# Hybrid trunk step with PEER experts: six slots for expert rows, eleven weight chunk buffers in one pool, and four heads' queries of layer 1 made a pass later

## The chip, the cores and the metric

The kernel runs on one core of a Trainium2 chip, in fp32. The metric is device time in microseconds (us), the median of the runs.

## The reference

Two token groups go through two layers: 256 prompt tokens and 32 sample tokens (8 sequences of 4), width 1024. Layer 0 mixes with a gMLP, layer 1 with a short convolution; each is followed by a PEER feed-forward, which is where most of the data comes from.

```
# layer 0 mixer                           # layer 1 mixer
z = gelu(x @ w_in); u, v = split(z)        B, C, h = split(x @ w_in)
v = layer_norm(v)                          z = C * h
y = (u * (tril(w_s) @ v + b_s)) @ w_out    y = (B * conv3(z)) @ w_out

# PEER, each layer, per token
q = (x @ w_query).reshape(8 heads, 2, 128)
s = q . sub_keys                           # 2 x 128 scores a head
top 16 of each half -> 256 sums -> top 16 -> idx = i1 * 128 + i2;  g = softmax
a = gelu(expert_u[idx] . x)                # 16 rows of 1024 a head
y = sum(g * a * expert_v[idx])
```

Before each mixer and each feed-forward stands an RMS norm, with a residual sum behind; a last norm follows. The outputs are the 288 rows, layer 0's normalised v of the sample rows, and the convolution buffers.

## The kernel before, in words

**Tiles and items.** The tokens are three tiles: 128, 128 and 32 rows. For a token, a head and one of its 16 experts the kernel needs one row of u and one of v, which lie side by side in DRAM (2048 floats). An *item* is one such row for each of the 128 partitions: one indirect load of 1 MiB, issued by GpSimd (POOL), L717. A tile of 128 tokens has 8 x 16 = 128 items, the small tile, folded four times over the partitions, 32; two layers make 576 items. An item goes into slot n % RING of `uvring`. VectorE multiplies its first half with the normed token and sums (`dot`, L1485), ScalarE takes gelu, multiplies by the gate and scales a small diagonal matrix (`weigh`, L1090 to L1102, in one of DIAGS places), TensorE adds the second half, so weighted, into two PSUM banks (`weigh`, L764, 4 matmuls, which the trace records as 8; L756 for the small tile). POOL loads item n into its slot when item n - RING is through TensorE (`v_tensor`). At a tile's end the sums are added to x (L1501) before TensorE starts the next tile's first item.

**Chunks and passes.** The dense matrices are cut in chunks of 1024 x 256 floats, 1 MiB each, numbered in the order of use: pass 0 is layer 0 for tile 0 (chunks 0 to 31), pass 1 layer 0 for tiles 1 and 2 (32 to 63), pass 2 and pass 3 the same for layer 1 (64 to 87 and 88 to 111). In layer 0 a pass has eight chunks for v, eight for u, eight for the output projection and eight for the queries; in layer 1 twelve for B, C and h, four for the output and eight for the queries. SyncE (SP) issues the chunk loads in that order, one after the other, L661 in `load_chunk`, each when the last use of its place is over. `plan_homes` gives each chunk a place: during pass 0 slots of the row ring that no item needs yet, later a ring of two buffers, `wring`. Six chunks of each layer have a place in `kept`; they are loaded in the layer's first pass and used again in its second. TensorE waits in `chunk(n, c)` for the landing. `blocks` makes 128 columns of a result transposed (eight matmuls, 16 records of the trace; a chunk serves two blocks): u, L775 at 160 or 128 tokens, the convolution's three parts (`bch`) and the queries (`q`), which go to `qT` in `arena`. The scores of a group of four half heads (`s`, L952) are made of `qT` and the sub-keys; ScalarE copies them to `scores` when VectorE has scanned the scores of the tile before at that place (`scanned`).

**The order.** `mixer_steps` lists the dense steps of a pass with costs in us and with what each must follow. `plan_steps` deals them to *turns*: turn p is item p, and each engine has so much room in a turn for such steps (`ROOM`, by layer and tile of the item); routing steps (the top-16 search on VectorE, `route`) have due turns (`due`, which depends on RING). Each engine runs, turn by turn, its item's work and the steps dealt to the turn. What stands at turn -1 runs ahead of all items: pass 0 with the first scores. So the order on each engine is fixed before the run; only semaphores decide when.

## Time and profile before

| what | value |
|---|---|
| runs | 1755.15, 1756.94, 1757.65 us, median 1756.94 |
| span of the profiled execution | 1753.3 us (its own time is not given; the median stands 3.6 us above the span) |
| TensorE busy | 1323.9 us (76%) |
| VectorE busy | 1082.8 us (62%) |
| ScalarE busy | 659.9 us (38%) |
| GpSimd busy | 626.8 us (36%) |
| moved by DMA | 719.43 MB, mean 410 GB/s |
| mean granted TensorE clock | 0.811 |
| chain that ended last | DMA 52%, TensorE 28%, VectorE 6%, ScalarE 6% |

Busy shares are averages over stages with different limits: what a change is worth in a stage is read from the stretches of the trace. In the chain of work that ended last, each piece is either work or the flight of a DMA; a row load's piece reaches from its issue to its landing and holds the time it stands behind other loads. TensorE's instructions are pipelined, so a busy TensorE need not be one at its peak.

### The profile page before, as it was taken

Reading aid. Unit: us, or ns where it says so; the run is one execution under the profiler, and the core shown is the slowest. Engines: PE = TensorE matmul, PEld = TensorE weight load, DVE = VectorE, ACT = ScalarE, POOL = GpSimd, SP = SyncE. Lnnn points to the kernel's source line nnn. Section 1 sums busy time; section 2 is a strip of 40 time slices with the busy share of each in tenths; the row PEclk is TensorE's granted clock in tenths of the full one; section 3 lists DMA queues with packets and bytes.
Section 4 is the critical chain, followed back from the end, with each engine's and each line's share of the span. In section 5 each row is a group of like instructions: output and inputs, shape, how many; then the busy total and the mean of one; then the engine's idle time right before and its main releaser. Section 6 shows DMA issues by size and latency. Waiting matters only on the chain.

```text
span 1753.3 us, 23627 instructions
## 1 busy us (share of the span) xinstructions
PE 1323.9 (76%) x8378; PEld 638.9 (36%) x8378; DVE 1082.8 (62%) x2636; ACT 659.9 (38%) x2139; POOL 626.8 (36%) x580
## 2 busy tenths in 40 slices
PE   8999998998868777886654688687896666766634
PEld 6995554654535433441110255244441111111100
DVE  1358578555755566556677756677567766666454
ACT  2125444234434223343443533336343433433343
POOL 0014333333333223333343443343344444434442
PEclk9999998998989978987655699898886766666755
DMA  9979999999999999999999999999999999999997
GB/s 346 412 328 403 410 421 421 421 421 421 408 422 421 421 420 421 421 419 421 422 411 421 395 421 421 421 420 414 421 397 419 421 421 421 421 421 416 422 410 301
DMA packets 101478, 719.43 MB, mean 410 GB/s; under 512 B 12272, under 2 KB 13040, under 8 KB 14416
## 3 DMA queue, kind: packets, MB, share of 16 engines
q0 software_dynamic: 82944, 604.02, 83.3%
q1 hardware_dynamic: 17616, 113.17, 15.8%
q8 instruction: 66, 1.08, 0.2%
q10 hardware_dynamic: 800, 0.74, 0.1%
q14 instruction: 52, 0.43, 0.1%
HBM read 716.36 MB, written 1.52 MB: 409 GB/s over the span
## 4 chain that ended last, share of the span: by engine, by line
DMA 52%; PE 28%; DVE 6%; ACT 6%; issue 3%; SPq 2%; POOL 1%; DVEq 0%; ACTq 0%; POOLq 0%
DMA uvring<-expert_uv_dram,idx 51%; PE psum L764 11%; PE psum L775 8%; DVE uvring L1485 5%; PE psum L931 4%; ACT diag L1102 1%; PE psum L819 1%; ACT wgt L1098 1%; POOL uvring L717 1%; DMA wring<-w_chunks_dram 1%; SPq L674 1%; ACT a_gelu L1090 1%; ACT L1090 1%; PE psum L952 1%; PE psum L783 1%
## 5 line engine op out<-in xcount | busy, mean ns | idle before, releaser
L1485 DVE SCALAR_TENSOR_TENSOR uvring<-uvring,xn 128x1024 f32<-128x1024 f32 x576 | 705.1, 1225 | 547.0 <-DMA uvring<-expert_uv_dram,idx 534.4
L717 POOL DMA_INDIRECT uvring<-expert_uv_dram,idx x576 | 626.6, 1088 | 1105.1 <-PE psum L764 845.8
L764 PE MATMUL psum<-uvring,diag 64*64 64x512 f32 x4096 | 685.0, 762 | 305.6 <-ACT diag L1102 281.6
L1090 ACT ACTIVATE a_gelu<-a_raw 128x1 f32<-128x1 f32 x576 | 116.6, 202 | 880.0 <-DVE uvring L1485 861.9
L764 PEld LDWEIGHTS psum<-uvring,diag 64*64 64x64 f32 x4096 | 131.8, 155 | 733.5 <-ACT diag L1102 630.8
L775 PEld LDWEIGHTS psum<-xT,wring 128*128 128x128 f32 x1408 | 188.3, 195 | 66.4 <-issue 59.8
L775 PE MATMUL psum<-xT,wring 128*128 128x160 f32 (+1 forms) x1408 | 206.4, 301 | 3.1 <-DMA wring<-w_chunks_dram 3.1
L1102 ACT ACTIVATE diag<-twin,wgt 128x64 f32<-128x64 f32 x512 | 178.1, 348 | 48.9 <-PE psum L764 1.5
L1098 ACT ACTIVATE wgt<-a_gelu,gate 128x1 f32<-128x1 f32 x576 | 169.7, 295 | 20.9
L756 PE MATMUL psum<-uvring,diag 128*32 128x256 f32 x512 | 67.2, 630 | 95.3 <-ACT diag L1102 83.7
L775 PEld LDWEIGHTS psum<-xT,kept 128*128 128x128 f32 x576 | 75.6, 197 | 24.2 <-issue 24.2
L775 PE MATMUL psum<-xT,kept 128*128 128x128 f32 (+1 forms) x576 | 82.1, 299 | 0.0
L756 PEld LDWEIGHTS psum<-uvring,diag 128*32 128x32 f32 x512 | 13.3, 142 | 149.2 <-ACT diag L1102 134.9
L931 PE MATMUL psum<-wring,arena 128*128 128x256 f32 x272 | 64.5, 392 | 2.0 <-DMA wring<-w_chunks_dram 2.0
L981 ACT ACTIVATE arena<-psum 128x128 f32<-128x128 f32 (+2 forms) x152 | 42.9, 282 | 55.9 <-PE psum L775 44.8
L931 PEld LDWEIGHTS psum<-wring,arena 128*128 128x128 f32 x272 | 51.7, 195 | 20.6 <-issue 9.7
L1485 DVE DVE_READ_ACCUMULATOR uvring<-uvring,xn 128x1 f32 x576 | 47.5, 83 | 0.0
L775 PE MATMUL psum<-xT,uvring 128*128 128x128 f32 x320 | 37.4, 276 | 3.2 <-DMA uvring<-w_chunks_dram 2.5
L1201 DVE FIND_INDEX8 ti<-tv,scores 128x8 uint32<-128x128 f32 x144 | 38.5, 285 | 0.0
L775 PEld LDWEIGHTS psum<-xT,uvring 128*128 128x128 f32 x320 | 36.4, 192 | 3.6 <-DMA uvring<-w_chunks_dram 2.7
L1090 ACT ACT_TABLE_LOAD x29 | 37.2, 1283 | 0.5
L866 PE MATMUL psum<-x,ident 64*128 64x512 f32 x48 | 29.2, 709 | 6.0 <-DVE kept L1384 6.0
(162 smaller groups left out, 862.8 us busy)
## 6 DMA issues: line engine op xcount, KB each, us to landing
wring<-w_chunks_dram SPq DMA_DIRECT2D x67, 1024.0 KB
uvring<-w_chunks_dram SPq DMA_DIRECT2D x20, 1024.0 KB, 12.3
kept<-w_chunks_dram SPq DMA_DIRECT2D x12, 1024.0 KB, 14.4
uvring<-expert_uv_dram,idx POOLq DMA_INDIRECT x576
uvring<-ln_gain_dram SPq DMA_DIRECT2D x1, 1024.0 KB, 26.3
uvring<-ln_bias_dram SPq DMA_DIRECT2D x1, 1024.0 KB, 27.8
keys<-sub_keys_dram SPq DMA_DIRECT2D x2, 512.0 KB, 17.2
arena<-w_chunks_dram SPq DMA_DIRECT2D x1, 1024.0 KB, 18.0
```

What stands on the lines that cost most here:

```text
L717: pool.indirect_dma_start(uvring[:, n % RING, :], None, expert_uv, bass.IndirectOffsetOnAxis(ap=idx[t][:, i:i + 1], axis=0),).then_inc(uv_ ...
L756: mm = nc.tensor.matmul(acc[32 * q:32 * q + 32, 0:256], diag[:, n % DIAGS, 0:32], row[:, D + 256 * q:D + 256 * (q + 1)], start=first, stop ...
L764: mm = nc.tensor.matmul(acc[64 * j:64 * j + 64, 512 * i:512 * (i + 1)], diag[64 * i:64 * i + 64, n % DIAGS, :], row[64 * i:64 * i + 64, D ...
L775: mm = nc.tensor.matmul(bank(key, WIDTH[n]), w[:, k, j * P:(j + 1) * P], act[:, k, 0:cols], start=(k == 0), stop=(k == KD - 1))
L866: nc.tensor.matmul(bank(k), matrix, values, start=True, stop=True).then_inc(group_done, 1)
L931: mm = nc.tensor.matmul(bank(key, WCOLS, ROWS[t]), act[:, h * KD + kk, LCOL[t]:LCOL[t] + ROWS[t]], w[:, kk, :], start=(h == 0 and kk == 0) ...
L981: nc.scalar.activation(out, bank(key, n, rows), func, scale=scale).then_inc(scalar_read, 1)
L1090: nc.scalar.activation(a_gelu[:, c:c + 1], a_raw[:, c:c + 1], ACT.Gelu_apprx_tanh).then_inc(gelu_done, 1)
L1098: nc.scalar.mul(wgt[:, c:c + 1], a_gelu[:, c:c + 1], gate[t][:, i:i + 1]).then_inc(weighed, 1)
L1102: nc.scalar.mul(diag[:, n % DIAGS, 0:32 if t == 2 else 64], fold[:, :] if t == 2 else twin[:, :], wgt[:, c:c + 1]).then_inc(diag_ready, 1)
L1201: V.max_index(where[:, at:at + 8], best[:, at:at + 8], values)
L1485: nc.vector.scalar_tensor_tensor(out=uvring[:, slot, 0:D], in0=uvring[:, slot, 0:D], scalar=1.0, in1=xn[t][:, :], op0=ALU.mult, op1=ALU.mu ...
```

## The change

- The row ring has six slots (RING), there are four diagonals (DIAGS) instead of eight, and `csn` shares the place of `state`. The program is built with 2048 bytes of each partition for the descriptors of POOL's DMAs (an argument that was not given before).
- `wring` (two buffers) and `kept` (six) are replaced by `wpool`, eleven buffers. Layer 0 keeps 11 chunks for its second pass, of 32; layer 1 keeps 15, of 24, some of them in buffers that another kept chunk has left. A chunk takes the place that is free earliest in the order of use. Pass 1's first two chunks go to `arena`.
- Queries of pass 2 are written where their scores will stand (`scores`), not to `qT`, and the tokens they are made of are transposed to `own_T`, the place of the gMLP's spatial weights.
- The last eight query blocks of pass 2 (four heads) are made during pass 3: blocks 8 to 11 behind its convolution block 5, blocks 12 to 15 behind block 15. Their four chunks are loaded then, and serve pass 3's own queries too.

```
-WRING = 2
+POOL = 11
...
-KEPT = [(1, 5, 12, 29, 30, 31), (1, 5, 9, 13, 17, 21)]
-KEEP = len(KEPT[0])
+KEPT = [(2, 3, 4, 5, 6, 7, 8, 28, 29, 30, 31), (0, 1, 2, 3, 4, 5, 6, 7, 8, 18, 19, 20, 21, 22, 23)]
+LATE = {8: (5, 8), 12: (15, 17)}
...
-RING = 7
-DIAGS = 8
+RING = 6
+DIAGS = 4
...
+def use_order():
+    order = list(range(PASS_CHUNK0[2] + 20))
+    for c in range(24):
+        order.append(PASS_CHUNK0[3] + c)
+        for b0, (behind, _) in LATE.items():
+            if c == behind // 2:
+                order += [PASS_CHUNK0[2] + 16 + b0 // 2, PASS_CHUNK0[2] + 17 + b0 // 2]
+    return order
...
+    for n in order:
+        first = max(p for p in PASS_CHUNK0 if p <= n)
+        c, l = n - first, 0 if n < PASS_CHUNK0[2] else 1
+        again = first in (PASS_CHUNK0[1], PASS_CHUNK0[3])
+        kept = c in KEPT[l]
+        if kept and again:
+            home[n] = home[n - first + PASS_CHUNK0[2 * l]]
+            continue
+        if n in (PASS_CHUNK0[1], PASS_CHUNK0[1] + 1):
+            h = ("arena", c)
+        elif first == 0 and kept:
+            h = ("pool", c - 2) if c < 9 else earliest([("pool", r) for r in range(7, POOL)])
         elif n < 24:
+            h = earliest([("slot", s) for s in (5, 2, 3, 4)] + [("pool", r) for r in range(7, POOL)])
+        elif first == 0:
+            h = ("slot", (0, 1, 4, 5)[c - 24])
         else:
+            h = earliest([("pool", r) for r in range(l == 0, POOL)])
...
+            for b0, (behind, scored) in LATE.items() if n == 3 else ():
+                for q in range(b0, b0 + 4) if b == behind else ():
+                    out.append(("PE", ("q", 2, q), 1.14 * KD * WIDTH[2] * mm, [("xT read", 1, "ffn", 0, 1)]))
+                    out.append(q_read(2, q))
+                if b == scored:
+                    out += scored_steps(1, 0, b0, 4)
...
-    for b in range(HP):
+    for b in range(min(LATE) if n == 2 else HP):
...
-    (1, 0): {"DVE": 1.2, "ACT": 1.5, "PE": 1.5},
+    (1, 0): {"DVE": 1.2, "ACT": 1.5, "PE": 1.6},
...
-        csn = sb("csn", [P, KD, SB, 2])
+        csn = state
...
+        own_T = wsm
...
                 if USES[HOME[n]][0] != n:
-                    wait_unused(sp, USES[HOME[n]][USES[HOME[n]].index(n) - 1])
+                    wait_unused(sp, last_use(USES[HOME[n]][USES[HOME[n]].index(n) - 1]))
...
-            for n in range(PREFETCHED, PASS_CHUNK0[2]):
+            for n in [*range(PREFETCHED, 28), 32, *range(28, 32), *range(33, PASS_CHUNK0[2])]:
                 load_chunk(n)
...
-            for n in range(PASS_CHUNK0[2], PASS_CHUNK0[4]):
+            for n in ORDER[PASS_CHUNK0[2]:]:
                 load_chunk(n)
...
-                    blocks(n, "q", b, xT, WIDTH[n])
+                    blocks(n, "q", b, own_T if n == 2 else xT, WIDTH[n])
...
+                                                  (qT if t else scores)[:, hp, 0:P], keys[:, hp, :],
...
+                    to = own_T if (l, which, t) == (1, "ffn", 0) else xT
...
-                    read(("q", n, b), qT[:, b, 0:WIDTH[n]], ACT.Copy, WIDTH[n])
+                    if n == 2:
+                        act.wait_ge(scanned, ROUTES.index(scanned_before(1, 0, b, 1)) + 1)
+                    read(("q", n, b), (qT if n % 2 else scores)[:, b, 0:WIDTH[n]], ACT.Copy, WIDTH[n])
...
-    nc = bacc.Bacc("TRN2", target_bir_lowering=False, num_devices=1)
+    nc = bacc.Bacc("TRN2", target_bir_lowering=False, num_devices=1, dynamic_dma_scratch_size=2048)
```

How SyncE's chunk loads stand before, from the place where pass 1 begins (`keys` is the load of layer 1's sub-keys, which divides pass 1 from pass 2):

```order
L661 DMA arena<-w_chunks_dram 128x2048
L661 DMA wring<-w_chunks_dram 128x2048 x25
L690 DMA keys<-sub_keys_dram 128x2048
L661 DMA wring<-w_chunks_dram 128x2048
L661 DMA kept<-w_chunks_dram 128x2048
L661 DMA wring<-w_chunks_dram 128x2048 x3
...
L661 DMA wring<-w_chunks_dram 128x2048 x20
```

And now, from the same chunk (32) on; its four `wpool` rows are the last chunks of pass 0, 28 to 31:

```order
L708 DMA arena<-w_chunks_dram 128x2048
L708 DMA wpool<-w_chunks_dram 128x2048 x4
L708 DMA arena<-w_chunks_dram 128x2048
L708 DMA wpool<-w_chunks_dram 128x2048 x19
L737 DMA keys<-sub_keys_dram 128x2048
L708 DMA wpool<-w_chunks_dram 128x2048 x33
```

Pass 1 loads 2 + 19 chunks where it loaded 1 + 25; behind the keys stand 33 loads where there were 42.

On TensorE, pass 2 before ended in this way, behind the scores of heads 2 and 3 (L764 is the items' work, L775 a query block, L952 a group of scores, L866 the next norm's gain):

```order
L952 MATMUL psum<-keys,arena 128x128 x4
L775 MATMUL psum<-xT,wring 128x128 x8
L764 MATMUL psum<-uvring,diag 64x512 x4
L775 MATMUL psum<-xT,wring 128x128 x8
L764 MATMUL psum<-uvring,diag 64x512 x8
L775 MATMUL psum<-xT,kept 128x128 x8
L764 MATMUL psum<-uvring,diag 64x512 x4
L775 MATMUL psum<-xT,kept 128x128 x8
L764 MATMUL psum<-uvring,diag 64x512 x12
L952 MATMUL psum<-keys,arena 128x128 x4
```

Now the norm's gain stands right behind those scores, and then only items up to the tile's end (L812 is the items' work, L1000 the scores, L914 the gain):

```order
L1000 MATMUL psum<-keys,scores 128x128 x4
L914 MATMUL psum<-x,ident 128x512
L812 MATMUL psum<-uvring,diag 64x512 x4
L914 MATMUL psum<-x,ident 128x512
L812 MATMUL psum<-uvring,diag 64x512 x216
L804 MATMUL psum<-uvring,diag 32x256 x128
```

And in pass 3 the first four of the moved blocks stand between convolution blocks (L823 on xT is a convolution block, L823 on wsm a moved query block):

```order
L823 MATMUL psum<-xT,wpool 128x160 x8
L812 MATMUL psum<-uvring,diag 64x512 x8
L823 MATMUL psum<-wsm,wpool 128x128 x8
L812 MATMUL psum<-uvring,diag 64x512 x4
L823 MATMUL psum<-wsm,wpool 128x128 x8
L812 MATMUL psum<-uvring,diag 64x512 x4
L823 MATMUL psum<-wsm,wpool 128x128 x8
L812 MATMUL psum<-uvring,diag 64x512 x4
L823 MATMUL psum<-wsm,wpool 128x128 x8
L812 MATMUL psum<-uvring,diag 64x512 x8
```

Blocks 8 to 11 moved from turns 200 to 204 to turns 304 to 307, blocks 12 to 15 from 207 to 211 to 324 to 328; pass 3's own steps stand up to 16 turns later for it.

## Rows read from the trace of the kernel before

**Rows 1.** The page, GB/s in 40 equal slices of the span (43.8 us each)
```profile
GB/s 346 412 328 403 410 421 421 421 421 421 408 422 421 421 420 421 421 419 421 422 411 421 395 421 421 421 420 414 421 397 419 421 421 421 421 421 416 422 410 301
```

**Rows 2.** The page: a DMA queue (packets, MB, share), and chunk loads by place
```profile
q0 software_dynamic: 82944, 604.02, 83.3%
...
wring<-w_chunks_dram SPq DMA_DIRECT2D x67, 1024.0 KB
uvring<-w_chunks_dram SPq DMA_DIRECT2D x20, 1024.0 KB, 12.3
kept<-w_chunks_dram SPq DMA_DIRECT2D x12, 1024.0 KB, 14.4
...
arena<-w_chunks_dram SPq DMA_DIRECT2D x1, 1024.0 KB, 18.0
```

**Rows 3.** Stretches: us; PE, PEld, DVE, ACT, POOL busy (xcount); PEclk, DMA share, GB/s
```profile
137.00:237.00 100.00, 94.67 (x659) 51.44 (x652) 71.73 (x194) 49.53 (x146) 42.47 (x36) 0.98 1.00 408
237.00:303.00 66.00, 56.82 (x348) 31.29 (x350) 51.70 (x118) 24.60 (x85) 24.96 (x22) 0.90 1.01 421
303.00:499.00 196.00, 177.76 (x1256) 106.73 (x1260) 118.56 (x292) 75.46 (x245) 72.74 (x64) 0.96 1.01 418
499.00:817.00 318.00, 236.39 (x1576) 125.07 (x1572) 184.02 (x454) 111.16 (x375) 109.27 (x101) 0.85 1.01 421
817.00:978.00 161.00, 90.41 (x520) 15.55 (x512) 111.02 (x264) 63.06 (x209) 64.43 (x65) 0.57 1.01 419
978.00:1301.00 323.00, 263.04 (x1769) 144.27 (x1762) 212.07 (x533) 133.27 (x432) 126.55 (x111) 0.90 1.01 416
1301.00:1708.00 407.00, 262.32 (x1308) 45.97 (x1306) 263.59 (x593) 155.94 (x519) 169.11 (x162) 0.66 1.01 417
```

**Rows 4.** Waits: engine, line, for whom: us in total, times, longest
```profile
SPq L661 <- PE psum L775: 818.5, 44, 219.1
...
PEld psum L764 <- ACT diag L1102: 630.8, 308, 5.1
...
ACT diag L1102 <- PE psum L764: 1.5, 4, 0.4
```

**Rows 5.** The chain's row loads in quiet stretches: start, us, what
```profile
1360.17 10.54 DMA uvring<-expert_uv_dram,idx
...
1544.70 12.79 DMA uvring<-expert_uv_dram,idx
...
1562.09 12.81 DMA uvring<-expert_uv_dram,idx
...
1578.61 13.68 DMA uvring<-expert_uv_dram,idx
```

**Rows 6.** The first rows: chain, and POOL's loads in time order
```profile
139.09 7.86 DMA uvring<-expert_uv_dram,idx
...
127.39 0.94 POOL L717 DMA_INDIRECT uvring<-expert_uv_dram,idx  x1 [0.84 <-PE psum L775]
137.72 0.94 POOL L717 DMA_INDIRECT uvring<-expert_uv_dram,idx  x1 [9.40 <-PE psum L764]
```

**Rows 7.** The chain: one query block of pass 2's width
```profile
591.32 1.98 PE psum L775 x16
```

**Rows 8.** Short stretches at five dips, and POOL's load behind a tile's change
```profile
904.00:910.00 6.00, 3.00 (x24) 0.78 (x24) 5.87 (x14) 3.16 (x6) 2.83 (x3) 0.50 0.96 382
986.00:1003.00 17.00, 14.47 (x94) 6.05 (x87) 14.78 (x34) 11.78 (x34) 8.06 (x7) 0.82 0.94 350
1200.00:1208.00 8.00, 8.00 (x67) 4.84 (x60) 5.88 (x16) 6.65 (x16) 3.52 (x4) 0.98 0.99 377
1305.00:1316.00 11.00, 8.69 (x60) 2.16 (x56) 8.30 (x25) 4.16 (x15) 6.60 (x6) 0.79 0.90 328
1674.00:1684.00 10.00, 4.26 (x36) 1.06 (x40) 7.62 (x14) 8.14 (x22) 4.94 (x5) 0.50 0.99 362
...
986.93 1.10 POOL L717 DMA_INDIRECT uvring<-expert_uv_dram,idx  x1 [6.76 <-PE psum L764]
```

More of the change, by code:

```diff
@@ L102, in scores_of, with last_use @@
+        assert free.get(h, -1) < at[n]
+        free[h] = at[PASS_CHUNK0[2 * l + 1] + c if kept else n]
+        home[n] = h
+        uses.setdefault(h, []).append(n)
+    return home, uses, order
+HOME, USES, ORDER = plan_homes()
+PREFETCHED = 9
+def last_use(n):
+    first = max(p for p in PASS_CHUNK0 if p <= n)
+    l = 0 if n < PASS_CHUNK0[2] else 1
+    return PASS_CHUNK0[2 * l + 1] + n - first if n - first in KEPT[l] else n
 def scores_of(l, t):
```

73 lines of the change are left out of this document (30 added, 43 removed).

## The prediction

> **What bounds the kernel now.** I read the page's slices first. From the fourth slice to the last but one the DMA engines are full and move 395 to 422 GB/s, in most slices 421, with the lowest at slices 11, 23 and 30 [rows 1]. The page's queue and issue lines say what is moved: 604 MB of expert rows in 576 indirect loads of 1 MiB each, and 67 + 20 + 12 + 1 = 100 loads of 1 MiB weight chunks [rows 2]. One MiB at 421 GB/s is 2.49 us. Then the stretches [rows 3]: where no chunk is loaded, 817 to 978 us, 65 row loads take 161 us, 2.48 us each, which is that rate; from 1301 to 1708 it is 2.51. Where chunks are loaded as well, a row takes longer, and the rate shows how many chunks went by: 303 to 499 us moves 81.9 MB, 78 loads, 64 of them rows and 14 chunks; 499 to 817 moves 128, of which 101 rows, the keys and 26 chunks; 978 to 1301 moves 128, of which 111 rows and 17 chunks. So past 237 us the kernel's time is its bytes. TensorE is second: 177.8 of 196 us busy from 303 to 499, less elsewhere. Only between 137 and 237 us (94.7 of 100) is it the limit itself [rows 3]. The loads that SyncE issues wait almost always for TensorE to free one of the two ring buffers [rows 4]; that costs nothing while rows keep the DMA engines full.
>
> How the row ring turns: in a quiet stretch, a load of the chain takes 12.79 us from 1544.70 to its landing, the next 12.81 from 1562.09, the next 13.68 from 1578.61; between a landing and the next start, 4.6 and 3.7 us, lie dot product, gelu, weight, diagonal and matmuls [rows 5]. A round of seven slots must take 7 x 2.49 = 17.4 us at the full rate; of it 3.7 to 4.6 us are work and some 13 us are landing, most of this queueing behind the other loads. The shortest landing in the chain is 7.86 us, with few loads ahead of it [rows 6].
>
> **The change, part by part.**
>
> *Fewer loads.* The new plan loads 86 chunks where the old one loaded 100. Pass 0 still loads 32. Pass 1 loads 21, not 26; pass 2 loads 20, not 24, since the last four query chunks (84 to 87) are left to pass 3; pass 3 loads these and 9 of its own, 13 where it was 18. That is 5 + 4 + 5 = 14 x 2.49 = 34.9 us of DMA time. What of it counts: the nine of layer 1 lie in stretches with TensorE at 236.4 of 318 and 263.0 of 323 us, so they count in full, 22.4 us. The five of pass 1 are chunks that are used until about 225 us, where TensorE is the limit; but the pool lets SyncE run up to six chunks ahead where the ring let it run two, so most of the freed DMA time is spent on later chunks. I count four: 10.0 us. Together 13 x 2.49 = **-32.4 us** (bounds -22.4, if TensorE eats all of pass 1, and -34.9). About 421 GB/s the Trainium skill says otherwise ("DMA: Bandwidth & Descriptors", Where 436 GB/s comes from): for HBM to SBUF the HBM side, about 358 GB/s, is said to bind. By that figure a chunk would be worth 2.93 us and the thirteen 38.1 us; the slices show 421 for most of this run, so the trace disagrees and decides.
>
> *Queries of layer 1 moved.* Eight blocks of eight matmuls over 128 tokens leave pass 2 (turns 200 to 211) and stand in pass 3 (turns 304 to 328). One block (16 records of the trace) takes 1.98 us [rows 7], so 15.8 us of TensorE go from a stretch with 82 us to spare to one with 60 us to spare [rows 3]. They cost nothing while spare time covers them; were it gone, up to 15.8 us. In turns 304 to 335, where they all stand, TensorE's load is the stretch's average of 263/111 = 2.4 us a row plus 0.5, 2.9; the DMA load there is some 38 MiB for 32 rows, 3.0 us a row. The cover is thin there, which the term on TensorE below takes in. The query reads now write into the scores' place and so wait on ScalarE for the scan of the tile before: the score reads behind them waited for the same scans already, so nothing. ScalarE's copy of the transposed tokens goes to another tile, nothing.
>
> *Deeper prefetch.* After the last scores of pass 1 all eleven buffers are free, and SyncE issues eleven loads at once (three before). Rows and chunks then share the engines and rows come at about half rate for some 55 us; no byte is added, and DMA stays full: 0. Before it, from turn 88 to 123, all chunks are already there, and rows alone run against TensorE's queries: DMA needs 2.49 us a row, TensorE's busy time in 303 to 499 is 177.8/64 = 2.78 [rows 3]. Over these 36 turns that would be 10 us above DMA, but the turns before carry more chunks and less TensorE work per load; sum over 237 to 499: 86 rows and 14.5 chunks need 250 us of DMA, TensorE 234.6. I take **+3** (0 to 10), the thin place in layer 1 included.
>
> *Six slots.* A round is now 6 x 2.49 = 14.9 us; less 4.6 of work leaves 10.3 us for a landing, against 7.86 needed [rows 5, 6]. So the full rate still holds in a quiet stretch, with 2.5 us to spare where there were 5. Where a stall is longer than that, the DMA engines run dry one load earlier. Such stalls are the change of tile, where TensorE waits for the sums and POOL 6.8 us for TensorE, and a few others: the five dips already lose 0.6, 2.9, 0.8, 2.4 and 1.4 us (1 - rate/421 of each stretch) [rows 8]. Each may lose 2.49 us more: 0 to 12.5. I take four in full, **+10**, as the dip at 1200 us has chunk loads beside it. The tile change at 512 us falls in the burst of eleven chunks: 0. At the start, the seventh load is issued at 127.39 us, in a slot of its own, and the eighth waits until 137.72, when the first row has been used [rows 6]. With six slots the seventh waits too, and the landing that the chain runs through at 139.09 moves one load back: **+2.5** (0 to 2.5).
>
> *Four diagonals for eight.* ScalarE may run four rows ahead of TensorE, not eight. It waited for TensorE there 1.5 us in all, and TensorE's weight loads waited 630.8 us for it [rows 4]; with six slots, of which two or more are landing, it can hardly be further ahead: 0 (up to 5 if it holds ScalarE's other reads in the dense stretch; queued behind a waiting diagonal are the copies that free TensorE's banks).
>
> *The start.* Chunk 27 now waits for chunk 23 and is issued near 104 us, not 98; TensorE uses it at about 118, with five loads of 2.49 between: hidden.
>
> *Smaller descriptor memory for POOL* (2048 bytes a partition). Queue 0 had 82944 packets for 576 loads, 144 each, 9 for each of 16 engines [rows 2]. If six loads fit, 0; that they don't is a rival.
>
> Sum: 1753.3 - 32.4 + 3 + 10 + 2.5 = 1736.4 us of span. The runs' median, 1756.94, is 3.6 above the profiled span; so 1740.0 us, a gain of 1.0%. A measurement of this kernel can tell about 0.2% from no change, 3.5 us.
>
> **Rivals.**
>
> A, *six slots are too few* (slower). If a landing at full rate really needs the 12.8 us of the quiet chain, and not 7.86, a round is 12.8 + 4.6 = 17.4 us for six loads, 2.90 us a row, 0.41 more on the 227 rows of 817 to 978 and 1301 to 1708: +93 us, 1833 in all. It decides from a needed landing of 10.8 us: there 0.08 us a row on 227 rows take back the 17 us that are left, 1757. For it: most landings of the chain in quiet stretches are over 12 us. Against: landings queue behind one another, so they fill whatever the ring grants; and 10.54 at 1360.17 and 7.86 at the start have been seen [rows 5, 6]. A milder form, 11 us needed, gives 2.60 us a row and 1765. Chance 0.09 for more than 10.9.
>
> B, *TensorE takes over* in pass 1 and again in turns 304 to 335: only layer 1's nine loads count and 10 us of the queries show: 1753.3 - 22.4 + 10 + 12.5 + 3.6 = 1757, no change. For it: 91% busy from 303 to 499. Against: 82% and less in layer 1. Chance 0.07. In half its strength it gives 1748.
>
> C, *POOL's descriptor memory holds fewer than six loads*, so that POOL waits for one to drain. With three in flight and a landing of 7.86 us a row takes 2.62 us, 0.13 more on 576: 1815 in all; with four or more it costs nothing. For it: POOL was never held so far, so the trace has no row for it. Against: 9 packets of each engine a load are little. Chance 0.03. The Trainium skill speaks against it: a descriptor is 16 bytes, and a 1 MiB load gives each engine 9 to read and 9 to write ("DMA: Bandwidth & Descriptors", Terms, and The descriptor swizzle); 2048 bytes would hold 128, or fourteen loads. The trace agrees on the 9.
>
> D, *no cost of slots at all*: queue depth was never needed, all 14 loads count: 1753.3 - 34.9 + 3.6 = 1722. Against: the dips show that it runs dry already. Chance 0.10.
>
> **How the numbers follow.** The forecast, 1740, with 1728 to 1751 for its own bounds, has 0.69. Range 1725 to 1757: it leaves out D's best part, A and C. The rest of the chance, 0.02, is for a part that I priced at nothing and that costs 10 us or so. Faster: forecast 0.69, D 0.10, two thirds of B, 0.84 with rounding; same 0.05, the rest of B and the edge of A; slower 0.11, A and C.
>
> **What would show it.** Right: 86 chunk loads and 14.7 MB less in queue 1; slices still at 421 between the dips; quiet stretches at 2.5 us a row, with landings of about 10.3 us in the chain in place of 13; dips at the tile changes deeper by up to a load each; layer 1's dense stretches shorter by 10 to 12 us each. Wrong: quiet stretches under 410 GB/s (A), TensorE over 95% busy with DMA below full past 237 us (B), POOL waiting for nothing that the profile names (C).

## The result, and the profile after

The changed kernel takes 1742.12 us (median of four runs, 1736.74 to 1744.45) where the kernel before takes 1757.29 (four runs, 1755.15 to 1757.65): ratio 0.9916, 95% interval 0.9898 to 0.9934. The forecast was 1740.0, with a range of 1725 to 1757. So the sum came out 2 us beside the measurement; the account below shows that three of its terms (the dips, pass 1's saved loads and TensorE's +3) did not, and that their errors cancel, which is luck.

The page of the changed kernel: span, GB/s in 40 equal slices (43.5 us each), packets, the two big queues, the chain's shares, and the issue lines (KB each, median us to landing).

```profile
span 1739.2 us, 23634 instructions
...
GB/s 342 412 278 386 381 421 410 401 420 395 397 416 421 419 421 421 419 419 422 418 405 422 396 422 420 416 422 405 407 421 385 423 421 416 421 421 417 422 408 321
DMA packets 99462, 704.75 MB, mean 405 GB/s; under 512 B 12048, under 2 KB 12816, under 8 KB 14192
...
q0 software_dynamic: 82944, 604.02, 84.5%
q1 hardware_dynamic: 15600, 98.49, 13.9%
...
DMA 49%; PE 31%; DVE 7%; ACT 7%; issue 3%; SPq 2%; POOL 1%; DVEq 0%; ACTq 0%; POOLq 0%
...
wpool<-w_chunks_dram SPq DMA_DIRECT2D x71, 1024.0 KB, 10.4
uvring<-w_chunks_dram SPq DMA_DIRECT2D x13, 1024.0 KB, 11.5
...
arena<-w_chunks_dram SPq DMA_DIRECT2D x2, 1024.0 KB, 16.6
```

71 + 13 + 2 = 86 chunk loads, as planned, and 719.43 - 704.75 = 14.7 MB less in all. The gain came from bytes alone: the mean rate fell from 410 to 405 GB/s. Beside [rows 1], seven of the nine slices from the fourth to the twelfth are lower (386, 381, 410, 401, 395, 397, 416); before, most of these stood at 421.

The same stretches as in [rows 3], of the changed kernel (us; PE, PEld, DVE, ACT, POOL busy with counts; clock, DMA share, GB/s):

```profile
137.00:237.00 100.00, 90.11 (x616) 47.09 (x614) 69.16 (x186) 45.11 (x137) 38.96 (x34) 0.97 0.97 388
237.00:303.00 66.00, 53.96 (x318) 28.78 (x318) 47.93 (x101) 26.09 (x84) 22.22 (x21) 0.87 1.00 414
303.00:499.00 196.00, 184.73 (x1280) 113.11 (x1280) 122.83 (x305) 75.87 (x249) 75.42 (x65) 0.96 1.00 405
499.00:817.00 318.00, 240.26 (x1520) 116.16 (x1512) 196.34 (x490) 114.69 (x385) 119.19 (x107) 0.82 1.01 420
```

Pass 1 (to some 500 us) moves 388, 414 and 405 GB/s where it moved 408, 421 and 418. Past 499 us the rate is as before, with 107 row loads in 318 us in place of 101: the chunks that are gone.

Four of the chain's row loads in the quiet stretch of layer 1 (start, us, what):

```profile
1423.39 10.35 DMA uvring<-expert_uv_dram,idx
...
1470.62 10.30 DMA uvring<-expert_uv_dram,idx
...
1485.50 10.33 DMA uvring<-expert_uv_dram,idx
...
1500.43 10.29 DMA uvring<-expert_uv_dram,idx
```

These landings are 10.3 us, against 12.8 in [rows 5], at the same rate. Over the chain's row loads between 1320 and 1650 us the median is 10.3 (8.7 to 12.9), before it was 12.8 (10.5 to 13.8). That is the figure of the prediction, 6 x 2.49 less 4.6.

**The account.** The dot product of item n begins each turn, so the trace gives each item's time, and the rate between two items tells how much was moved. Four items cut the run in three. These are the windows between items 0, 32, 128 and 575 in the trace of before:

```profile
124.50:218.60 94.10, 89.73 (x661) 53.13 (x659) 69.11 (x202) 44.74 (x137) 38.36 (x33) 0.98 1.00 407
218.60:512.50 293.90, 260.37 (x1758) 150.40 (x1754) 188.58 (x452) 114.18 (x365) 110.40 (x99) 0.94 1.01 419
...
512.50:1744.90 1232.40, 859.70 (x5224) 331.88 (x5228) 783.36 (x1854) 472.19 (x1566) 472.85 (x442) 0.75 1.01 416
```

And between the same items in the changed kernel:

```profile
124.70:226.40 101.70, 94.05 (x678) 55.54 (x678) 68.06 (x194) 44.49 (x137) 36.84 (x33) 0.97 0.97 389
226.40:517.60 291.20, 260.65 (x1745) 151.14 (x1743) 188.73 (x452) 114.02 (x367) 111.54 (x98) 0.94 1.00 408
...
517.60:1730.70 1213.10, 855.62 (x5224) 332.73 (x5228) 783.92 (x1862) 471.56 (x1566) 474.64 (x443) 0.75 1.01 415
```

The first stretch is 7.6 us longer, the second 2.7 shorter, the third 19.3 shorter. Each length can be taken apart: the packets that landed in it, in MiB, times 2.49 us (one MiB at 421 GB/s), and the rest, the *shortfall*, time in which the DMA engines moved less than that. For the kernels of this study (counted from each trace's packets, one trace each):

| kernel, slots | items 0 to 128: us | MiB | shortfall | of it 0 to 32 | of it 64 to 128 | items 128 to 575: us | MiB | shortfall |
|---|---|---|---|---|---|---|---|---|
| before, 7 | 388.0 | 154.0 | 4.5 | 3.1 | 1.3 | 1232.4 | 489.5 | 13.1 |
| changed, 6 | 392.9 | 151.0 | 16.8 | 7.9 | 6.8 | 1213.1 | 480.6 | 16.1 |
| the same, once more (again) | 388.5 | 151.2 | 12.0 | 6.6 | 5.4 | 1215.3 | 480.4 | 18.7 |
| before with 6 (ring6) | 399.0 | 154.6 | 13.8 | 9.0 | 3.0 | 1235.4 | 488.9 | 17.8 |
| changed with 7 (ring7) | 385.5 | 151.3 | 8.6 | 7.0 | 1.6 | 1209.7 | 480.7 | 12.5 |
| ring7, six chunks kept (l0less) | 385.2 | 153.0 | 4.1 | 3.1 | 0.6 | 1210.8 | 480.4 | 14.3 |
| changed, all queries in pass 2 (nolate) | 390.1 | 151.0 | 14.1 | 8.1 | 4.7 | 1224.4 | 484.6 | 17.3 |
| ring7, half of u (half_ring7) | 383.7 | 151.4 | 6.6 | 5.9 | 0.6 | 1211.2 | 480.6 | 14.1 |
| changed with 8 (ring8) | 387.0 | 153.8 | 3.9 | 3.6 | 0.2 | 1209.3 | 480.2 | 13.4 |
| changed, half of u (half_after) | 393.1 | 151.8 | 15.1 | 7.4 | 7.6 | 1210.2 | 479.8 | 15.1 |
| changed, half of u and queries (halfq_after) | 381.9 | 150.2 | 7.7 | 6.1 | 0.6 | 1215.3 | 481.3 | 16.4 |

Behind item 128 the change takes 8.9 MiB away (22.2 us) and adds 3.0 us of shortfall. In items 0 to 128 it takes 3.0 MiB away (7.5 us) and adds 12.3 us of shortfall. So in pass 1 the time saved on bytes was lost again, and more. Not all of the 12.3 us is the sixth slot's: with seven slots the same chunk plan still has 4.1 us more shortfall than before (8.6 against 4.5), nearly all in items 0 to 32. The rest, 8.2 us here and 3.4 in the second trace, comes with six slots. How that can happen shows at 405 us of the changed kernel. TensorE's instructions there, in order of time (start, us, what):

```profile
405.94 1.98 PE L812 MATMUL psum<-uvring,diag 64*64 64x512 f32 x8 [2.30 <-ACT diag L1154]
407.85 4.33 PE L979 MATMUL psum<-wpool,arena 128*128 128x256 f32 x16
412.12 1.07 PE L831 MATMUL psum<-wpool,arena 128*32 128x256 f32 x16
413.12 1.95 PE L812 MATMUL psum<-uvring,diag 64*64 64x512 f32 x16
```

POOL's row loads meanwhile, and then the rate of the 12 us that follow:

```profile
408.23 0.94 POOL L764 DMA_INDIRECT uvring<-expert_uv_dram,idx  x1 [2.54 <-PE psum L812]
414.51 1.70 POOL L764 DMA_INDIRECT uvring<-expert_uv_dram,idx  x1 [5.35 <-PE psum L812]
...
414.00:426.00 12.00, 9.20 (x54) 2.70 (x46) 10.22 (x24) 7.09 (x19) 7.88 (x6) 0.87 0.88 323
```

Two dense blocks of the output projection stand in a row, 5.3 us; no row is used up in that time, POOL waits 5.35 us for a slot, and 323 GB/s follow. The changed kernel with seven slots (ring7, below) reaches this place 5.7 us earlier (item 96 at 423.8, here at 429.5) and shows no dip:

```profile
408.00:420.00 12.00, 7.90 (x45) 2.04 (x44) 9.77 (x22) 7.29 (x19) 4.99 (x4) 0.75 1.02 423
```

Not each such place dips in each run. The shortfall in items 88 to 95, where this one stands, is 2.7 us here, 3.1 in nolate and 3.7 in half_after, but 0.3 in the changed kernel's second trace, and none with seven slots or in ring6. The dips at items 103 to 110 and 121 to 124, where the query blocks stand, are in both traces of the changed kernel.

### The profile page after: what moved, and what is told of

Its sections match the earlier page's. It is cut to its first block, busy times and chain, and to the rows that moved or that the text cites. A ratio compares the mean times of both kernels' runs of the same rounds, so it can differ in the third digit from the quotient of the medians.

```text
span 1739.2 us, 23634 instructions
## 1 busy us (share of the span) xinstructions
PE 1323.9 (76%) x8378; PEld 642.5 (37%) x8378; DVE 1082.4 (62%) x2636; ACT 658.7 (38%) x2139; POOL 627.6 (36%) x580
## 2 busy tenths in 40 slices
DMA packets 99462, 704.75 MB, mean 405 GB/s; under 512 B 12048, under 2 KB 12816, under 8 KB 14192
## 4 chain that ended last, share of the span: by engine, by line
DMA 49%; PE 31%; DVE 7%; ACT 7%; issue 3%; SPq 2%; POOL 1%; DVEq 0%; ACTq 0%; POOLq 0%
DMA uvring<-expert_uv_dram,idx 48%; PE psum L812 12%; PE psum L823 9%; DVE uvring L1537 6%; PE psum L979 3%; ACT diag L1154 2%; PE psum L867 2%; ACT wgt L1150 2%; ACT a_gelu L1142 1%; SPq L721 1%; POOL uvring L764 1%; PE psum L914 1%; ACT L1142 1%; PE psum L831 1%; PE psum L1000 1%
## 5 line engine op out<-in xcount | busy, mean ns | idle before, releaser
L764 POOL DMA_INDIRECT uvring<-expert_uv_dram,idx x576 | 627.4, 1089 | 1092.5 <-PE psum L812 854.5
L812 PE MATMUL psum<-uvring,diag 64*64 64x512 f32 x4096 | 681.5, 760 | 293.3 <-ACT diag L1154 272.1
L812 PEld LDWEIGHTS psum<-uvring,diag 64*64 64x64 f32 x4096 | 130.8, 153 | 720.9 <-ACT diag L1154 627.7
L823 PEld LDWEIGHTS psum<-xT,wpool 128*128 128x128 f32 x1824 | 246.2, 197 | 79.7 <-issue 72.7
L823 PE MATMUL psum<-xT,wpool 128*128 128x160 f32 (+1 forms) x1824 | 268.7, 303 | 2.1 <-DMA wpool<-w_chunks_dram 2.1
L979 PE MATMUL psum<-wpool,arena 128*128 128x256 f32 x320 | 78.0, 400 | 1.8 <-DMA wpool<-w_chunks_dram 1.8
L979 PEld LDWEIGHTS psum<-wpool,arena 128*128 128x128 f32 x320 | 62.4, 200 | 22.9 <-issue 11.8
L1030 ACT ACTIVATE arena<-psum 128x160 f32<-128x160 f32 (+2 forms) x120 | 34.1, 284 | 36.0 <-PE psum L823 28.8
L823 PEld LDWEIGHTS psum<-wsm,wpool 128*128 128x128 f32 x256 | 33.9, 213 | 12.2 <-issue 12.2
L823 PE MATMUL psum<-wsm,wpool 128*128 128x128 f32 x256 | 36.8, 303 | 0.0
L914 PE MATMUL psum<-x,ident 64*128 64x512 f32 x48 | 26.6, 650 | 5.6 <-DVE wpool L1436 5.5
L1253 DVE FIND_INDEX8 ci<-cv,pick 128x8 uint32<-128x256 f32 x72 | 29.3, 418 | 0.0
L1501 DVE TENSOR_TENSOR x<-x,psum 128x256 f32<-128x256 f32 (+1 forms) x24 | 9.9, 414 | 30.5 <-PE psum L979 30.1
## 6 DMA issues: line engine op xcount, KB each, us to landing
keys<-sub_keys_dram SPq DMA_DIRECT2D x2, 512.0 KB, 17.1
```

The lines of the kernel that those rows point to most:

```text
L764: pool.indirect_dma_start(uvring[:, n % RING, :], None, expert_uv, bass.IndirectOffsetOnAxis(ap=idx[t][:, i:i + 1], axis=0),).then_inc(uv_ ...
L812: mm = nc.tensor.matmul(acc[64 * j:64 * j + 64, 512 * i:512 * (i + 1)], diag[64 * i:64 * i + 64, n % DIAGS, :], row[64 * i:64 * i + 64, D ...
L823: mm = nc.tensor.matmul(bank(key, WIDTH[n]), w[:, k, j * P:(j + 1) * P], act[:, k, 0:cols], start=(k == 0), stop=(k == KD - 1))
L914: nc.tensor.matmul(bank(k), matrix, values, start=True, stop=True).then_inc(group_done, 1)
L979: mm = nc.tensor.matmul(bank(key, WCOLS, ROWS[t]), act[:, h * KD + kk, LCOL[t]:LCOL[t] + ROWS[t]], w[:, kk, :], start=(h == 0 and kk == 0) ...
L1253: V.max_index(where[:, at:at + 8], best[:, at:at + 8], values)
```

## The experiments

Each kernel ran beside the kernel before on the same chip; ratios are against those runs, with 95% intervals.

**ring6: six slots.** The kernel before, with all its 100 chunk loads in their order; the seventh slot's place serves as a third chunk buffer while pass 0 runs. It is not quite the slot alone: `due` depends on RING, so from turn 11 on the routing steps are dealt one turn later, and 69 of TensorE's steps ahead of turn 128 with them. The changed kernel and ring7 differ from each other in the same way, and no run takes the two apart.

```
-RING = 7
+RING = 6
...
-    places = [("slot", s) for s in (5, 6, 2, 3, 4)] + [("ring", r) for r in range(WRING)]
-    queries = [("slot", s) for s in (0, 1, 4, 5, 6)]
+    places = [("slot", 5), ("ring", 2)] + [("slot", s) for s in (2, 3, 4)] + [("ring", r) for r in range(WRING)]
+    queries = [("slot", s) for s in (0, 1, 4, 5)] + [("ring", 2)]
...
-        wring = sb("wring", [P, WRING, KD, WCOLS])
+        wring = sb("wring", [P, WRING + 1, KD, WCOLS])
...
```

> The kernel before with six slots for rows, and nothing else changed: the seventh slot's place serves as a third chunk buffer for the chunks that used that slot, so all 100 chunk loads stay, in the same order. My theory (six slots cost time mostly in the dense start and in pass 1, where the changed kernel lost 5 us by item 128 in spite of its saved chunks, and 2 to 5 us at the tile changes): 1757 + 12 to 20, so 1769 to 1777, with item 128 reached 10 to 15 us later than in the kernel before and quiet stretches still at 2.5 us a row. Rival (the loss in pass 1 comes from the new order of loads and the new plan, not from the slots): 1757 to 1762, item 128 at most 3 us later.

Measured: 1770.7 us (1768.98 to 1777.5), before 1755.37; ratio 1.0098 (1.0073 to 1.0122). Six slots cost 15.3 us, near the 12.5 that the prediction gave to start and dips together, but elsewhere: item 128 comes 12.4 us late (1.4 of it is there at item 0), item 575 15.4. In the quiet stretch nothing is lost. Window and two of the chain's landings of ring6 there:

```profile
1450.00:1650.00 200.00, 135.63 (x640) 22.14 (x640) 131.95 (x301) 76.30 (x257) 80.01 (x80) 0.65 1.01 419
...
1451.89 10.65 DMA uvring<-expert_uv_dram,idx
...
1476.20 11.18 DMA uvring<-expert_uv_dram,idx
```

**ring5: where a ring becomes too short.** The same with one slot fewer and one spare chunk buffer more.

```
-RING = 7
+RING = 5
...
-        wring = sb("wring", [P, WRING, KD, WCOLS])
+        wring = sb("wring", [P, WRING + 2, KD, WCOLS])
...
```

> The kernel before with five slots, all 100 loads kept in their order (two spare chunk buffers take the place of the two slots). A round at the full rate is 12.5 us; less 4.6 of work leaves 7.8 for a landing. My theory (a landing needs 7 to 8 us): quiet stretches just lose the full rate, 2.5 to 2.6 us a row, and every stall shows: 1755 + 45 to 90. Rival A of the prediction (a landing needs over 10 us): 2.9 us a row in quiet stretches, 1755 + 150 or more. Rival the other way (a landing needs 6 us or less): quiet stretches stay at 2.49 and the loss is 20 to 30 us.

Measured: 1838.68 us (1834.63 to 1846.45), before 1756.54; ratio 1.0483 (1.0453 to 1.0513). The same 200 us, and landings of the chain in ring5:

```profile
1450.00:1650.00 200.00, 129.99 (x616) 21.76 (x616) 130.44 (x320) 71.05 (x243) 77.62 (x77) 0.66 1.00 404
...
1467.32 9.44 DMA uvring<-expert_uv_dram,idx
...
1481.36 7.83 DMA uvring<-expert_uv_dram,idx
...
1493.56 7.99 DMA uvring<-expert_uv_dram,idx
```

77 rows in 200 us are 2.60 us each: here the quiet stretch itself is slower; these three landings are 7.8 to 9.4 us, the median of the chain's between 1320 and 1650 us is 8.7. 5 x 2.49 = 12.5 less 4.6 leaves 7.9 us, and that no longer holds the rate; 10.3 us, with six, does. So what a landing needs at full rate lies between these, well under rival A's 12.8. The quiet stretches explain only a small part of the 82 us, though: 0.1 us on 227 rows are some 25. The shortfall of items 0 to 128 alone grows by 31 us (35.5 against 4.5), and that behind item 128 by 50 (63.0 against 13.1), so more than half of the loss lies outside the quiet stretches.

**small: diagonals and descriptor memory alone.** The kernel before with four diagonals and 2048 bytes a partition for POOL's descriptors.

```
-DIAGS = 8
+DIAGS = 4
...
-    nc = bacc.Bacc("TRN2", target_bir_lowering=False, num_devices=1)
+    nc = bacc.Bacc("TRN2", target_bir_lowering=False, num_devices=1, dynamic_dma_scratch_size=2048)
```

> The kernel before with four diagonals for eight and with 2048 bytes of descriptor memory, seven slots and 100 chunk loads as before. My theory: neither binds, 1757 within 3 us. Rival (ScalarE is held by the fourth diagonal where TensorE is dense, or POOL waits for descriptor memory): 3 to 10 us slower, seen as waits of the diagonal for TensorE well over the 1.5 us of before, or as POOL loads longer than 1088 ns in the mean.

Measured: 1755.7 us (ten runs, 1754.15 to 1757.25), before 1755.37 (13 runs); ratio 1.0 (0.999 to 1.0009). Neither costs anything that shows, in a ring of seven slots. The wait of ScalarE for a free diagonal, in small:

```profile
ACT diag L1102 <- PE psum L764: 1.1, 3, 0.4
```

It is no longer than the 1.5 us of [rows 4].

**ring7: the new plan with seven slots.** The changed kernel, one slot more and one pool buffer less; each layer keeps one chunk less (10 and 14), so 88 chunks are loaded.

```
-POOL = 11
+POOL = 10
...
-KEPT = [(2, 3, 4, 5, 6, 7, 8, 28, 29, 30, 31), (0, 1, 2, 3, 4, 5, 6, 7, 8, 18, 19, 20, 21, 22, 23)]
+KEPT = [(2, 3, 4, 5, 6, 7, 28, 29, 30, 31), (0, 1, 2, 3, 4, 5, 6, 7, 18, 19, 20, 21, 22, 23)]
...
-RING = 6
+RING = 7
...
```

> The changed kernel with seven slots and ten pool buffers: 10 chunks of layer 0 and 14 of layer 1 are kept, so 88 are loaded, two more. My theory: + 5 us for the two loads, and back what six slots cost, 12 to 18 us: 1728 to 1735, faster than both. Rival (slots cost nothing here, bytes are all): 1742 + 5 = 1747.

Measured: 1730.91 us (1729.36 to 1731.28), before 1755.37; ratio 0.9859 (0.9842 to 0.9875). It is faster than both kernels, 24.5 us under before, though it loads two chunks more than the changed kernel. Between its items 0, 32, 128 and 575:

```profile
125.50:223.00 97.50, 92.58 (x681) 55.76 (x681) 68.95 (x203) 44.72 (x137) 41.57 (x34) 0.98 0.97 391
223.00:510.90 287.90, 257.39 (x1741) 149.50 (x1739) 188.58 (x452) 114.03 (x365) 107.47 (x98) 0.94 1.01 419
...
510.90:1720.70 1209.80, 854.44 (x5224) 328.67 (x5228) 782.77 (x1854) 471.58 (x1566) 478.42 (x442) 0.76 1.01 417
```

The middle stretch is back at 419 GB/s, at the rate of before and with 2.5 MiB less, and shorter than before by 6.0 us for it. Up to turn 128 ring7 has the plan of before, step for step.

**ring8: does an eighth slot bring more?** Against ring7 one more slot, nine buffers, 9 and 13 chunks kept, 90 loads.

```
-POOL = 10
+POOL = 9
...
-RING = 7
+RING = 8
...
```

> The changed kernel with eight slots and nine pool buffers: 9 and 13 chunks kept, so 90 are loaded, two more than with seven slots. My theory: the seventh slot was worth some 15 us on top of its two loads because six leave 2.5 us to spare in a round; the eighth adds spare time where little is short, worth 3 to 6 us, against 5 for its loads: 1729 to 1734, no faster than seven. Rival (every slot is worth the same): 1720.

Measured: 1730.91 us (1729.37 to 1732.02), before 1756.54; ratio 0.9855 (0.9839 to 0.9872). The same as with seven, by medians of four within 3 us of each other: what it wins in depth is no more than its two more loads cost, 5.0 us at most, and less if layer 0's chunk costs nothing (l0less).

**nolate: the moved queries alone undone.** Pass 2 makes all its queries itself, and layer 1 keeps 11 chunks, not 15; 90 loads.

```
-KEPT = [(2, 3, 4, 5, 6, 7, 8, 28, 29, 30, 31), (0, 1, 2, 3, 4, 5, 6, 7, 8, 18, 19, 20, 21, 22, 23)]
+KEPT = [(2, 3, 4, 5, 6, 7, 8, 28, 29, 30, 31), (0, 1, 2, 3, 4, 5, 6, 7, 8, 22, 23)]
...
-LATE = {8: (5, 8), 12: (15, 17)}
+LATE = {}
...
```

> The changed kernel with all queries of layer 1's first tile in pass 2 again; the pool of eleven can then keep 11 chunks of layer 1, not 15, so 90 chunks are loaded, not 86. My theory (layer 1's time is its bytes): 4 x 2.49 = 10 us slower than the changed kernel, 1752. Rival (the moved queries cost TensorE time in pass 3 that the saved loads only just pay for): 1740 to 1746.

Measured: 1747.5 us (1745.71 to 1748.4), before 1755.37; ratio 0.9952 (0.9936 to 0.9969). The whole lies between theory and rival. Its window from item 128 to item 575 decides:

```profile
513.80:1738.20 1224.40, 863.59 (x5224) 337.32 (x5228) 784.11 (x1862) 471.71 (x1566) 474.81 (x443) 0.75 1.01 415
```

1224.4 us against 1213.1 and 1215.3 in the changed kernel's two traces: 9 to 11 us for 4.0 to 4.2 MiB, which are 10.0 to 10.5 us. A load saved in layer 1 counts in full, and the query blocks moved for it cost nothing that shows. What blurred the total is pass 1, whose plan is the same up to turn 200: item 128 came at 513.8 us here, at 517.6 in the changed kernel.

**again: the changed kernel a second time**, to see how much pass 1 scatters.

> The changed kernel once more, beside the others on this chip, and a second trace of it. My theory: 1742 within 3 us of median, and item 128 reached within 5 us of the first trace's 517.6, since the kernel with all queries in pass 2 has the same order of work up to there and reached it at 513.8. Rival: 517.6 again within 1 us, so that the 3.9 us between those two are the plan's.

Measured: 1739.35 us (1736.44 to 1741.91), before 1756.54; ratio 0.9906 (0.9888 to 0.9924). Item 128 at 511.8 us, 5.8 earlier than in the first trace, a little more than the 5 that I had allowed; so the 3.9 us between nolate and the first trace are scatter, and the rival (517.6 again) falls. With six slots one kernel spreads over 8 us (1736.44 to 1744.45 in eight runs); ring7's four lie within 2. In both traces the shortfall of items 0 to 128 is 12 us or more. With seven slots item 128 scatters too: 512.5 in before, 513.8 in small, whose plan is the same.

**l0less: are pass 1's saved loads worth anything?** ring7, with only six chunks of layer 0 kept: chunks 36 to 39 are loaded again, early, while pass 0 leaves the DMA engines room.

```
-KEPT = [(2, 3, 4, 5, 6, 7, 28, 29, 30, 31), (0, 1, 2, 3, 4, 5, 6, 7, 18, 19, 20, 21, 22, 23)]
+KEPT = [(2, 3, 28, 29, 30, 31), (0, 1, 2, 3, 4, 5, 6, 7, 18, 19, 20, 21, 22, 23)]
```

> Seven slots and ten pool buffers as before, but layer 0 keeps 6 chunks and not 10: 92 loads, four more, all of pass 1 (chunks 36 to 39). My theory now (pass 1 is held by TensorE and by the turn of the row ring, so that the chunks saved there bought nothing): item 128 stays at 508 to 514 us and the time at 1731 within 3. Rival (my step of the prediction: four of pass 1's saved chunks count at 2.49 us each): item 128 at 521, 1741.

Measured: 1730.53 us (1730.05 to 1733.26), before 1755.46; ratio 0.9858 (0.9841 to 0.9874). Four loads more cost nothing. The table tells part of why. More than half of them land before item 0 (2.6 MiB more there), so items 0 to 128 see 1.7 MiB more, not 4. Of these 0.9 fall in items 0 to 32, where ring7 had 7.0 us of shortfall and this kernel 3.1. The other 1.1 fall in items 32 to 64, where DMA is full (0.1 us of shortfall in ring7), and that stretch does take 3.4 us more; items 64 to 128 take 2.1 less, with 0.4 MiB and 1.1 us of shortfall less. So a load counts where DMA is full and not elsewhere, which agrees with these two traces; but their difference is within what one kernel scatters.

**half_before and half_ring7: does TensorE hold pass 1?** In before and in ring7, each u block of pass 1 makes four of its eight matmuls; half of u's sum for tiles 1 and 2 is left out. What the queries of these tiles are made of changes with it, so other expert rows are read, as many.

```
+                last = KD // 2 if (name, n) == ("u", 1) else KD
-                for k in range(KD):
+                for k in range(last):
...
-                                          start=(k == 0), stop=(k == KD - 1))
+                                          start=(k == 0), stop=(k == last - 1))
```

> The kernel before with half of the matmuls of pass 1's sixteen u blocks left out (four of eight for each block, so u of tiles 1 and 2 lacks half of its sum): 16 x 1.2 = 19 us less TensorE work between turns 31 and 70. My theory: before was held by its bytes from about turn 32 on, so item 128 comes 0 to 4 us earlier. Rival (TensorE held pass 1 already): 8 us or more.

> The same matmuls left out of the kernel with seven slots and ten buffers, 88 loads. My theory: with its chunks saved, pass 1 is held by TensorE, so item 128 comes 5 to 10 us earlier than 510.9, and the time falls by as much. Rival (bytes and ring alone): under 2 us.

Measured: half_before 1756.41 us (ten runs, 1754.11 to 1758.74), before 1755.46 (13 runs), ratio 1.0002 (0.9992 to 1.0011): no gain, item 128 at 515.3 us, 2.8 later than before. half_ring7 1729.98 (1729.63 to 1731.12), ratio 0.9852 (0.9835 to 0.9868), against ring7's 0.9859: some 1 us, within the noise, item 128 at 508.5, 2.4 earlier, not 5 to 10. So my theory that TensorE's work holds pass 1 falls for the kernels with seven slots, as far as the u blocks (turns 31 to 70) go; v, output and query blocks were not cut there. From item 32 to 128 ring7 has only 1.7 us of shortfall (8.6 less 7.0): it is bound by its bytes.

**half_after and halfq_after: the same cut with six slots.** The first is half_before's edit on the changed kernel. The second also halves pass 1's query blocks; half of their sums for tiles 1 and 2 is left out. Both read other expert rows, as many.

```
+                last = KD // 2 if name in ("u", "q") and n == 1 else KD
```

> The changed kernel with four of eight matmuls in each u block of pass 1 (half of u's sum for tiles 1 and 2 is left out). Counted from the traces so far, the DMA engines fall short of 421 GB/s by 16.8 and 12.0 us between the first item's and item 128's dot product with six slots (the changed kernel's two traces), 8.6 with seven slots, 4.5 before. Theory 1: the six-slot ring runs dry where TensorE's dense blocks hold a row back; with half of u gone the shortfall in items 0 to 128 falls by 2 to 5 us and the time is 1735 to 1739, ratio about 0.989. Rival: the shortfall comes from the landing alone, whatever TensorE does: 1739 to 1743, ratio 0.9905 to 0.992, as with seven slots, where the same cut brought about 1 us.

> The changed kernel with four of eight matmuls in each u block and each query block of pass 1 (half of both sums for tiles 1 and 2 is left out; the expert rows that are read are then others, as many). Theory 1: the query blocks stand in items 64 to 123, where the changed kernel's two traces fall 7 and 5 us short of 421 GB/s; with both cuts the shortfall in items 0 to 128 is 5 to 9 us, as with seven slots, and the time 1731 to 1736, ratio 0.986 to 0.988. Rival: the shortfall does not depend on TensorE's work: 1739 to 1743.

Measured: half_after 1737.69 us (1736.78 to 1742.0), before 1755.11, ratio 0.9905 (0.9888 to 0.9921), as the changed kernel's 0.9906 and 0.9916. The time lies in theory 1's range and the ratio in the rival's; the shortfall in items 0 to 128 decides: it is 15.1 us, not 2 to 5 lower, so the u blocks are not what drains the ring. halfq_after 1734.94 (1731.78 to 1738.69), ratio 0.9890 (0.9873 to 0.9906). The time is within theory 1's range, the ratio just outside. The intervals of all three overlap, so the time alone proves nothing, but the trace shows the place. From item 64 to item 128, first the changed kernel:

```profile
323.70:517.60 193.90, 177.64 (x1258) 104.52 (x1256) 118.01 (x291) 75.81 (x247) 79.86 (x67) 0.97 1.00 406
```

then halfq_after:

```profile
321.70:506.20 184.50, 158.68 (x1084) 83.46 (x1083) 117.88 (x291) 74.83 (x243) 71.48 (x66) 0.94 1.01 420
```

The shortfall there falls from 6.8 (and 5.4 in the second trace) to 0.6 us. Not all of it is the cut's: 2.7 of the 6.8 stand in items 88 to 95, ahead of the first query block (turn 96), and in the second trace they are missing without a cut. In items 96 to 127, where the query blocks stand, the four six-slot traces of the changed plan with whole queries fall short by 2.9, 4.8, 1.6 (nolate) and 3.8 us (half_after), halfq_after by 0.6. That half_after reads other rows too and keeps its shortfall speaks against the rows as the cause. So with six slots TensorE's query blocks hold rows back and drain the ring, for some 1 to 4 us; with seven and the same blocks the shortfall is 1.5 us (ring7, no better than nolate) or 0.5 (l0less). This rests on one trace of halfq_after. In items 0 to 32 neither cut helps (7.4 and 6.1 us), but none of the cut blocks stands there.

## Why the prediction was right, and where it was not

*Layer 1's nine loads count in full, -22.4: right.* 8.9 MiB less between items 128 and 575 are 22.2 us, and nolate gives 9 to 11 us for four of them. The split is not the 10 to 12 us for each dense stretch that I named: items 128 to 256 take 16 us less, with 6.8 to 7.0 MiB less, and items 288 to 416 take 4 less, with 2.0 to 2.4.

*Moved queries, diagonals, descriptor memory, the burst of eleven loads at 0: right as far as shown.* small measures two of them together at 0.3 us, with an interval of some 1.7 us to either side; nolate leaves nothing for the queries. Their new places (`scores`, `own_T`) and `csn` were in no run apart. From item 128 to item 144 the burst takes 17.1 us more than before, from item 128 to item 160 it is 2.1 less: rows wait, bytes do not. Chunk 27 was hidden: item 0 comes at 124.7 us, before at 124.5.

*A round of six slots leaves 10.3 us for a landing, and that holds the rate: right*, by ring6, and by the changed kernel's quiet stretch, 10.3 us on the chain at 419 GB/s. That rules out rival A: the full rate holds with 10.3 us for a landing, so it doesn't need 10.8 or more. (That landings of up to 12.9 us are still seen on the chain shows only that they queue.) Rival B falls in its cause: with u halved nothing is won (half_before, half_ring7, half_after), and nolate shows nothing of the 10 us for queries in layer 1; yet its result for pass 1, that only layer 1's nine loads count, is what the changed kernel's traces show, by another cause. Rival C falls by small. Rival D is nearly what ring7 does (ratio 0.9859), but only with the seventh slot back.

*Six slots cost +10 at five dips, +2.5 at the start: the amount nearly right, by luck, the place wrong.* ring6 measures 15.3 us, 12.4 of it before item 128. Behind item 128 the shortfall grows by 4.7 us in ring6 and by 3.0 and 5.6 in the changed kernel, not by 10, and not at the five dips: counted over the same items, these lose 8.1 us in before, 7.9 in ring6 and 5.7 in both traces of the changed kernel, where the dip at 1305 us is gone. The start's +2.5 isn't separated: items 0 to 7 fall short by 2.0 us in before and 4.6 in ring6, but by 2.7 in the changed kernel and 4.6 in ring7. Two of the dips of [rows 8] in the changed kernel (there 986 and 1674 us):

```profile
975.30:992.30 17.00, 14.89 (x96) 5.89 (x88) 15.16 (x37) 10.03 (x29) 7.77 (x7) 0.79 0.95 357
...
1659.70:1669.70 10.00, 4.30 (x37) 1.06 (x40) 7.84 (x14) 8.14 (x22) 4.58 (x5) 0.50 0.98 354
```

357 and 354 GB/s, where before had 350 and 362: not a load deeper. I had taken the stalls that already showed as the only ones, and they were not. POOL's waits in the kernel before, first in pass 1 (170 to 510 us), then in the quiet stretch (1320 to 1600; us in total, times, longest):

```profile
POOL uvring L717 <- PE psum L764: 194.9, 73, 10.0
...
POOL uvring L717 <- PE psum L764: 159.6, 100, 6.1
```

The step that failed is the reading "with 2.5 us to spare where there were 5" for the quiet stretch alone. POOL waits for a slot in the same share of both stretches (57%), but in pass 1 in fewer and longer pieces: 2.7 us in the mean (194.9/73) and up to 10.0, against 1.6 in the quiet stretch. Seven slots cover more of these stalls than six, and much of the cost stands where before showed nothing: in the changed kernel in items 88 to 111 (5.2 and 3.4 us; before 0.0, ring7 1.5). In ring6 it stands partly where before dipped a little: items 16 to 23 (1.2 became 4.5) and 112 to 119 (1.3 became 3.0).

*Pass 1: four of five saved loads, -10.0, and TensorE +3: wrong.* The trace has 3.0 MiB less there, 7.5 us, and no gain is left: items 0 to 128 take 4.9 us more (0.5 in the second trace). With seven slots the same plan wins 2.5 us there. Part of the step is wrong by l0less: four of these loads more cost nothing in all, most of them beside pass 0 or in items 0 to 32, where DMA isn't full. Those past item 32 count (ring7: 2.5 MiB, 6.0 us). The +3 stood for TensorE's busy time; halving u shows that its busy time in turns 31 to 70 is not the bound. What was shown of TensorE in pass 1 is the length of its stalls against the ring's depth, at the query blocks.

So start and pass 1 were put at -4.5 and came out at +5.1 (-0.7 in the second trace); the rest at -12.4 and came out at -19.3 (-17.1). The errors have opposite signs, and the total lies between: that it came within 2 us of the forecast is luck. Span against span the gain is 14.1 us (1753.3 to 1739.2), where the sum had 16.9. The 3.6 us that it added for the median are too many as well: the lowest run of before, 1755.15 us, stands 1.8 above that span, which is what every run on record stands above its own; the rest of the 3.6 is scatter. One reading of [rows 1] was off: slice 4 (403) is lower than slice 11 (408). The rule of the Trainium skill that I had weighed, 358 GB/s for HBM to SBUF ("DMA: Bandwidth & Descriptors", Where 436 GB/s comes from), is not borne out by these runs either: the slices stand at 421. The Trainium skill's page "Perfetto Trace Analysis", Roofline, reads that figure as the share of a core whose neighbour is active too, and lets a single active core have about 435; with that this trace agrees.

*What stays open.* Items 0 to 32. Of the 6.7 us that ring6 takes longer there than before (100.8 against 94.1), 5.9 are shortfall. The changed kernel (101.7 and 100.6) takes 4.2 and 3.1 us more than ring7 (97.5), but with 1.3 MiB more, which are 3.2 us. The slots show most clearly in items 16 to 23: all six-slot traces fall short by 3.6 to 5.5 us there, all seven-slot ones by 1.2 to 2.5. TensorE's v blocks of pass 1 stand there (turns 12 to 29), again two dense blocks in a row ahead of a row's work. First the chain of the changed kernel from 135 to 240 us by lines, then two of the blocks:

```profile
by line: PE psum L867 25.9%; DMA uvring<-expert_uv_dram,idx 21.1%; PE psum L812 17.6%; DVE uvring L1537 6.9%; PE psum L831 6.7%; PE psum L823 2.9%; issue 2.7%; DVE xn L1396 2.6%; PE psum L894 1.9%; POOL uvring L764 1.5%; ACT L1037 1.2%; ACT
...
162.81 5.41 PE L867 MATMUL psum<-arena,xT 128*128 128x256 f32 x16
168.14 1.07 PE L831 MATMUL psum<-arena,xT 128*32 128x256 f32 x16
```

The v blocks (L867) are the largest part of that chain, and no run cut them; that they drain the six-slot ring there, as the query blocks do later, is likely but not shown. That ring7 takes 97.5 us in items 0 to 32 and before 94.1, with the same slots and the same plan, is open too; half_ring7 and l0less take 96.0, so part of it is scatter. The one turn by which `due` moves the steps with six slots was never tested apart. Nor was a ring of six with pass 1's dense blocks cut finer, so that items come between them.

## What to carry to other kernels

Judge a ring's depth in the stretch with the longest stalls of its consumer, not in the quiet one alone: depth that is spare in the quiet stretch may be just what hides dense blocks elsewhere (here the query blocks), and then the trace of before can show no dip at the place where the cost will come. When a buffer can serve either as a ring slot or as a cache, price both in the same unit: here the seventh slot was worth 11 to 15 us (its gain of 8 to 10 us and the one or two loads paid for it), the eighth at most the 5 us of the two chunks it displaced, and one kept chunk 2.5 us where DMA is full and little or nothing where it isn't. And take a total that comes out right apart by stretches before believing its terms.
